# The pooled output projection of the first block in three fp32r products of halves, in place of plain fp32 products

## The chip, the cores and the metric

One core of one Trainium2 chip runs the whole program. The metric is the device time of one execution in microseconds (us). Times of single instructions come from one profiled execution on the chip.

## The reference

Two blocks run one after the other over 256 tokens of width 1024, each with two layers, all in fp32. The change lies in the first block, whose layer is (cut):

```python
proj = xm @ w_in[l]
q, k, v, u_pool, ga, gp = jnp.split(proj, splits, axis=-1)
...
attn = blocked_bidirectional_gqa(q, k, v) @ w_attn_o[l]
pool = multiscale_pool(u_pool, pool_mix_w[l], pool_scale[l]) @ w_pool_o[l]
merged = jax.nn.sigmoid(ga) * attn + jax.nn.sigmoid(gp) * pool
x = x + g1[:, None, :] * (merged @ w_out[l])
xf = modulate(rms_norm(x, norm_ffn_w[l]), sh2, sc2)
x = x + g2[:, None, :] * peer_ffn(xf, w_query[l], sub_keys[l], expert_u[l], expert_v[l])
```

`multiscale_pool` ends with four products of 128x128 (`pool_mix_w`, one for each group of 128 features) and a scale; its 512 features then go through `w_pool_o` (512 x 1024). That last product is the one that changes. `peer_ffn` picks 16 experts a token for each of 8 heads out of 16384 and gathers their rows.

## The kernel before

Activations lie transposed: 128 features on the partitions, 256 tokens along the free axis, so a matrix of width 1024 is 8 tiles of 128x256 (`KD` = 8). The weights of a layer come as one stream of 128x128 tiles, eight tiles (512 KB) to a chunk, into a ring of 7 chunks (`RING`). SyncE loads a chunk when TensorE has used the one 7 before it (`w_used`). The last 17 chunks of a layer don't go through the ring but into `spare` places, tiles whose first use is over by then (`load_spare`), and four (`EARLY`) into the rows' buffer.

A projection g fills one of four PSUM banks of `G` (`bank(g)`) and is taken out (evacuated) by another engine before the bank is used again (`bank_free_1`, `g_free`). It is made in one of two ways:

- `project` (L684): plain fp32 matmuls of the ring's tiles with the fp32 activations, `kt` of them. In the trace an fp32 matmul is two records.
- `project_halved` (L696, the products in `halved_products`, L354): weights and activations are each cut in a high half, rounded to fp32r, and a low half, the remainder, and three fp32r matmuls are added: high by high, high by low, low by high. ScalarE writes `w_high` of a whole chunk (`high_half`, L342), VectorE subtracts it from the ring's chunk into `w_low` (`low_half`, L350). There are three places for these halves (`PARTS`), so ScalarE waits until TensorE has used the halved chunk three before.

`HALVING_1` is the list of which projections are halved and so which chunks. `Halves.ahead(eng, g)` lets an engine cut all halved chunks up to two behind the last chunk of projection g. Each engine's order is written out by hand: it calls `ahead` at the head of each iteration.

The order of a layer on TensorE: 32 input projections (`ORDER_1`, halved but for v, mixed with the attention), chunks 0 to 31; four mixing products (`G_MIX`, one plain matmul each) of the `pooled` tiles that GpSimd made; eight pooled output projections (`G_POOLO`, four k-steps each, plain; tiles 260 to 291, in chunks 32 to 36); `ada_part`, 8 thin matmuls with one column; eight attention output projections (`G_ATTO`, halved, eight k-steps); eight of `w_out` (`G_OUT`, halved); the norm, the first expert queries, and the expert stage.

Around the change the other engines do this:

- ScalarE copies the mixing products out with the pool's scale (`mixed`, L933, shown as rows<-G,par), makes the high halves of the eight attention tiles (`x_high`, L992), then the `w_high` that `ahead` asks for.
- VectorE runs a loop over the eight pooled output projections: `ahead`, `x_low` of attention tile j (L1268), the merge of gate and projection j (L1290, shown as rows<-gates,G), which frees the bank, and one ada step (L450 or L452), a multiply-add of 128x1024 of the modulation weights. Layer 0 has ada steps here; layer 1 has none left (`STEPS` is 32, all taken in the input projections).
- TensorE's first attention output projection waits for `x_low` tile by tile.
- The places: `pooled` and `mixed` lie in the rows' buffer, behind them the padded inputs of the pool (`upad`, `win`). The first four `spare` places lie on those, too.

Of the kernel before, what the change touches and what calls it, by code (L numbers as in the profile page):

```python
# [17 lines left out]
ALU = mybir.AluOpType  # L18
ACT = mybir.ActivationFunctionType
AX_X = mybir.AxisListType.X  # L20
F32 = mybir.dt.float32
# [356 lines left out]
def halved_pair(pe, w, T, sem, halving, outs, high, low, kt, ready, full, place=UNSHIFTED):  # L378
# [5 lines left out]
    for ks in (range(split), range(split, kt)):  # L384
        for turn, out in enumerate(outs):
# [15 lines left out]
            if ks[-1] == kt - 1:  # L401
# [7 lines left out]
                    + [((4, False), G_POOLO + _j) for _j in range(KD)]  # L409
# [48 lines left out]
def first_layer(nc, layer, io, T, sem, rows, run, nxt):  # L458
# [55 lines left out]
    with block:  # L514
        @block.sync
        def _(sp):
# [15 lines left out]
            def load_spare(first, last):  # L532
                for n in range(first, last):
                    sp.dma_start(T["spare"][n], T["stream1"][layer * CHUNKS_1 + RING_CHUNKS + n]
                                 ).then_inc(run["c_then_spare_loaded"], 16)
# [9 lines left out]
            for at in range(EARLY[0] - RING, EARLY[0]):  # L545
                sp.wait_ge(sem["w_used"], at - RING + 1)
                load_chunk(sp, T["stream1"], layer, CHUNKS_1, ring, sem["w_loaded"], at)
                if at == EARLY[0] - RING:
                    sp.wait_ge(sem["pooled"], 4)
                    load_spare(0, 4)  # L550
                if at == EARLY[0] - RING + 2:
                    sp.wait_ge(sem["x_low_ready"], 2 * KD)
                    load_spare(4, 6)
                if at == EARLY[0] - RING + 3:
                    evacuated_1(sp, g_free, G_POOLO + KD - 1)
                    load_spare(6, 8)
# [105 lines left out]
        def _(pe):  # L662
# [33 lines left out]
            def project_halved(g, high, low, ready=None):  # L696
                bank_free_1(pe, g_free, g)
                halved_products(pe, w, T, sem, HALVING_1, G[:, bank(g), 0:S], high, low, KD, ready
                                ).then_inc(g_full, 1)
# [100 lines left out]
            for j in range(KD):  # L800
                project(G_POOLO + j, lambda k: mixed[:, k, :], 4)
# [127 lines left out]
        def _(act):  # L929
# [117 lines left out]
            for g in range(4):  # L1047
                copy_out(G_MIX + g, mixed[:, g, :], scale=columns(par, PAR_1, "pool_scale")[:, g:g + 1])
            act.wait_ge(sem["o_ready"], HEADS)
# [99 lines left out]
        def _(dve):  # L1149
# [123 lines left out]
            for i, what in enumerate(ORDER_1):  # L1273
# [8 lines left out]
                if i - 3 in q_at:  # L1282
                    maxima(q_at[i - 3])
            for j in range(KD):
# [1319 lines left out]
def second_layers(nc, io, T, sems, run):  # L2604
# [4 lines left out]
    with nc.Block() as block:  # L2609
# [22 lines left out]
        def _(dve):  # L2632
# [8 lines left out]
           "diag_ready", "y_copied", "dve_chain", "high_ready", "low_ready", "x_high_ready", "x_low_ready", "x2_high")  # L2641
# [41 lines left out]
def program(nc, io):  # L2683
    with ExitStack() as ctx:
# [34 lines left out]
        with ExitStack() as first:  # L2719
# [54 lines left out]
            with ExitStack() as scope_halves:  # L2774
# [4 lines left out]
                sb1("pooling_place", 6144)  # L2779
# [257 lines left out]
```

## Time and profile before

| what | us |
|---|---|
| median of 3 runs | 3457.57 (3456.27 to 3458.91) |
| the profiled execution | 3455.86 |
| its span, first to last instruction | 3454.1 |
| TensorE busy | 3175.4 (92%) |
| VectorE busy | 2464.8 (71%) |
| ScalarE busy | 1665.6 (48%) |
| GpSimd busy | 1142.0 (33%) |

The profile has 48307 instructions. Layer 0 of the first block lasts until about 964 us, layer 1 until about 1883, the second block the rest. In the 40 slices of the page TensorE is at nine tenths or more in nearly all of the second block. The DMA engines move about 409 GB/s in the expert stages and less elsewhere. A record of TensorE overlaps the next one, since its end is modelled; the distance between the starts tells what one costs. An entry such as "[5.61 <-ACT x_high L992]" says how long the engine was idle before the instruction, and what it waited for last.

### The profile page before, as it was taken

What the parts mean: (1) busy time and instruction counts of PE and PEld (TensorE: products, weight loads), DVE (VectorE), ACT (ScalarE), POOL (GpSimd) and SP (SyncE); (2) the same over time, 40 slices, a digit from 0 to 9 for tenths busy, and PEclk for the clock granted to TensorE, in tenths of its full rate; (3) what the DMA queues carried; (4) which work ended last, traced back from release to release, by engine and by line L of the source; (5) the groups of instructions that cost most, each with busy time, mean ns of one, the idle gap of its engine ahead of it and who ended that gap; (6) DMA issues with size and microseconds to landing.
All of it is one profiled execution on the core that took longest, in us unless ns stands there. A gap on an engine that the chain in (4) does not pass through costs nothing. (4 is left out here: it accounts for less than half of the span.)

```text
span 3454.1 us, 48307 instructions
## 1 busy us (share of the span) xinstructions
PE 3175.4 (92%) x16922; PEld 2418.2 (70%) x16922; DVE 2464.8 (71%) x4772; ACT 1665.6 (48%) x3730; POOL 1142.0 (33%) x1243
## 2 busy tenths in 40 slices
PE   6998999987789798988977999999999999999999
PEld 6995544443289764444423888999988888999988
DVE  7876776666577666677764877767787867867686
ACT  3743343333365433333333555756554655756553
POOL 1306677777613167777773000002000000002000
PEclk8999999999999899999999999999999999999999
DMA  8798999999966799999997554444455554444455
GB/s 309 241 352 346 409 409 409 408 408 409 394 245 201 286 409 409 409 408 407 406 409 291 176 183 141 136 144 137 159 187 185 182 184 141 136 141 140 159 187 161
DMA packets 258286, 936.98 MB, mean 271 GB/s; under 512 B 29312, under 2 KB 30720, under 8 KB 257792
## 3 DMA queue, kind: packets, MB, share of 16 engines
q0 software_dynamic: 161280, 587.27, 43.3%
q1 hardware_dynamic: 96768, 346.62, 30.4%
q8 instruction: 138, 2.26, 0.3%
q14 instruction: 100, 0.82, 0.1%
HBM read 932.73 MB, written 1.05 MB: 270 GB/s over the span
## 5 line engine op out<-in xcount | busy, mean ns | idle before, releaser
L876 PE MATMUL M<-rows,diag 128*128 128x512 f32 x2048 | 965.1, 609 | 179.1 <-DMA rows<-in_expert_v_dram,expert 164.5
L1398 DVE CUSTOM_DVE_ANT_0 rows<-rows,G 128x1024 f32<-128x1024 f32 x512 | 615.5, 1219 | 408.0 <-DMA rows<-in_expert_u_dram,expert 319.4
L876 PEld LDWEIGHTS M<-rows,diag 128*128 128x128 f32 x2048 | 368.1, 191 | 724.2 <-DMA rows<-in_expert_v_dram,expert 383.1
L350 DVE TENSOR_TENSOR w_low<-ring,w_high 128x1024 fp32r<-128x1024 f32 x560 | 689.9, 1235 | 246.5 <-ACT w_high L342 227.5
L342 ACT ACTIVATE w_high<-ring 128x1024 fp32r<-128x1024 f32 x560 | 590.6, 1057 | 251.9 <-PE G L433 134.0
L595 POOL DMA_INDIRECT rows<-in_expert_u_dram,expert x512 | 484.0, 945 | 326.8 <-DVE expert L1381 139.4
L595 POOL DMA_INDIRECT rows<-in_expert_v_dram,expert x512 | 482.3, 942 | 189.6 <-issue 117.0
L369 PE MATMUL G<-x_halves,w_high 128*128 128x256 f32 x1360 | 400.7, 295 | 4.1 <-DVE w_low L350 3.9
L372 PE MATMUL G<-x_halves,w_low 128*128 128x256 f32 x1360 | 386.0, 284 | 0.0
L1106 ACT ACTIVATE diag<-const,weight 128x128 f32<-128x128 f32 x512 | 197.0, 394 | 258.0 <-PE M L876 257.1
L371 PE MATMUL G<-x_halves,w_high 128*128 128x256 f32 x1104 | 314.5, 285 | 0.0
L1093 ACT ACTIVATE gelu<-hid 128x2 f32<-128x2 f32 x256 | 51.7, 202 | 483.4 <-DVE hid L1398 482.8
L369 PEld LDWEIGHTS G<-x_halves,w_high 128*128 128x128 f32 x1360 | 262.0, 193 | 12.2 <-issue 10.7
L1675 POOL TENSOR_TENSOR gates<-gates 128x256 f32<-128x256 f32 x30 | 22.2, 739 | 740.7 <-ACT xs L2079 740.7
L372 PEld LDWEIGHTS G<-x_halves,w_low 128*128 128x128 f32 x1360 | 261.9, 193 | 0.0
L433 PE MATMUL G<-ff_halves,w_high 128*128 128x512 f32 x672 | 239.3, 400 | 0.0
L433 PE MATMUL G<-x_halves,w_high 128*128 128x512 f32 x616 | 224.7, 403 | 12.9 <-DVE w_low L350 12.1
L433 PE MATMUL G<-attn_halves,w_high 128*128 128x512 f32 x616 | 221.6, 396 | 0.0
L371 PEld LDWEIGHTS G<-x_halves,w_high 128*128 128x128 f32 x1104 | 213.9, 194 | 0.9
L369 PE MATMUL G<-x_high,w_high 128*128 128x256 f32 x608 | 180.3, 296 | 15.6 <-DVE x_low L1268 14.1
L435 PE MATMUL G<-ff_halves,w_low 128*128 128x256 f32 x672 | 188.2, 280 | 0.0
L371 PE MATMUL G<-x_low,w_high 128*128 128x256 f32 x608 | 174.8, 287 | 0.0
(416 smaller groups left out, 6126.4 us busy)
## 6 DMA issues: line engine op xcount, KB each, us to landing
ring<-in_stream_dram SPq DMA_DIRECT2D x612, 512.0 KB, 3.5
ada_ring<-in_ada_stream_dram POOLq DMA_DIRECT2D x80, 512.0 KB, 5.2
rows<-in_ada_stream_dram POOLq DMA_DIRECT2D x16, 512.0 KB, 16.3
rows<-in_stream_dram SPq DMA_DIRECT2D x16, 512.0 KB, 7.4
rows<-in_expert_u_dram,expert POOLq DMA_INDIRECT x512, 10.5
rows<-in_expert_v_dram,expert POOLq DMA_INDIRECT x512, 10.5
ada_ring<-in_stream_dram SPq DMA_DIRECT2D x8, 512.0 KB, 6.7
spare<-in_stream_dram SPq DMA_DIRECT2D x6, 512.0 KB, 10.3
```

The costliest lines, as they stand in the source:

```text
L342: act.activation(T["w_high"][:, place.part(n), :], T["ring"][:, slot, :], ACT.Copy).then_inc(sem["high_ready"], 1)
L350: dve.tensor_tensor(T["w_low"][:, part, :], T["ring"][:, place.slot(chunk, slots), :], T["w_high"][:, part, :].bitcast(F32), ALU.subtract) ...
L369: mm = pe.matmul(out, T["w_high"][:, part, tile], high(k), start=(k == 0), stop=False)
L371: pe.matmul(out, T["w_high"][:, part, tile], low(k), start=False, stop=False)
L372: mm = pe.matmul(out, T["w_low"][:, part, tile], high(k), start=False, stop=(k == kt - 1))
L433: mm = pe.matmul(out, T["w_high"][:, part, tile], pair(k), start=(k == 0), stop=False)
L435: pe.matmul(out[:, 0:S], T["w_low"][:, part, tile], pair(k)[:, 0, :], start=False, stop=False)
L595: pool.indirect_dma_start(buf[:, n % SLOTS, :], None, table, bass.IndirectOffsetOnAxis(ap=T["expert"][:, r, k:k + 1], axis=0)).then_inc(la ...
L876: mm = pe.matmul(M[:, 2 * t + half, :], T["diag"][:, n % 4, :], T["v_rows"][:, n % SLOTS, half * 512:(half + 1) * 512], start=(h == 0 and ...
L1093: act.activation(T["gelu"][:, r, k0:k0 + PAIR], T["hid"][:, r, k0:k0 + PAIR], ACT.Gelu).then_inc(sem["gelu_done"], 1)
L1106: act.activation(T["diag"][:, n % 4, :], ident, ACT.Copy, scale=T["weight"][:, r, k:k + 1]).then_inc(sem["diag_ready"], 1)
L1398: dve.tensor_tensor_reduce(row, row, TOKENS, 1.0, 0.0, ALU.mult, ALU.add, T["hid"][:, r, k:k + 1]).then_inc(sem["u_used"], 1)
```

## The change

The pooled output projections become halved ones. Their weights' chunks 32 to 35 join the halved chunks (36 was one already, since the attention output projection shares it). The mixed tiles get halves: ScalarE makes `mixed_high` of a group right behind its copy, once the copy has ended, and VectorE makes `mixed_low` of the four groups ahead of its loop. TensorE's first pooled output projection waits for `mixed_low` tile by tile. Both halves lie where `upad` and `win` were, and so on the first two spare places; these first four spare loads move on the SyncE queue from behind the first of the last seven ring chunks before the early ones to behind the fourth.

```diff
@@ HALVING_1
-                    + [((4, False), G_POOLO + _j) for _j in range(KD)]
+                    + [((4, True), G_POOLO + _j) for _j in range(KD)]
@@ sync
-                if at == EARLY[0] - RING:
-                    sp.wait_ge(sem["pooled"], 4)
-                    load_spare(0, 4)
                 if at == EARLY[0] - RING + 2:
                     sp.wait_ge(sem["x_low_ready"], 2 * KD)
                     load_spare(4, 6)
                 if at == EARLY[0] - RING + 3:
                     evacuated_1(sp, g_free, G_POOLO + KD - 1)
+                    load_spare(0, 4)
                     load_spare(6, 8)
@@ tensor
-            def project_halved(g, high, low, ready=None):
+            def project_halved(g, high, low, ready=None, kt=KD):
                 bank_free_1(pe, g_free, g)
-                halved_products(pe, w, T, sem, HALVING_1, G[:, bank(g), 0:S], high, low, KD, ready
+                halved_products(pe, w, T, sem, HALVING_1, G[:, bank(g), 0:S], high, low, kt, ready
                                 ).then_inc(g_full, 1)
...
             for j in range(KD):
-                project(G_POOLO + j, lambda k: mixed[:, k, :], 4)
+                project_halved(G_POOLO + j, lambda k: T["mixed_high"][:, k, :], lambda k: T["mixed_low"][:, k, :],
+                               (lambda k: pe.wait_ge(sem["mixed_low_ready"], k + 1)) if j == 0 else None, 4)
@@ scalar
             for g in range(4):
                 copy_out(G_MIX + g, mixed[:, g, :], scale=columns(par, PAR_1, "pool_scale")[:, g:g + 1])
+                evacuated_1(act, g_free, G_MIX + g)
+                act.activation(T["mixed_high"][:, g, :], mixed[:, g, :], ACT.Copy).then_inc(sem["mixed_high_ready"], 1)
@@ vector
+            for g in range(4):
+                dve.wait_ge(sem["mixed_high_ready"], g + 1)
+                dve.tensor_tensor(T["mixed_low"][:, g, :], mixed[:, g, :], T["mixed_high"][:, g, :].bitcast(F32),
+                                  ALU.subtract).then_inc(sem["mixed_low_ready"], 1)
             for j in range(KD):
                 halves_of.ahead(dve, G_POOLO + j)
@@ program
-                sb1("pooling_place", 6144)
+                sb1("pooling_place", 2048)
+                T1["mixed_high"], T1["mixed_low"] = sb1("mixed_high", 4, S, dt=F32R), sb1("mixed_low", 4, S, dt=F32R)
+                sb1("padded_place", 2048)
```

The order on VectorE in layer 0, from the last w_low of the input projections (chunk 31) to the third merge, before:

```order
L350 TENSOR_TENSOR w_low<-ring,w_high 128x1024 [waits high_ready_a,ada_step_or_dta_ready_a]
L452 SCALAR_TENSOR_TENSOR query<-ada_ring,c_act,query 128x1024 [waits ada_loaded1]
L452 SCALAR_TENSOR_TENSOR query<-ada_ring,c_act,query 128x1024 [waits ada_loaded2,ada_step_or_dta_ready_a]
L452 SCALAR_TENSOR_TENSOR query<-ada_ring,c_act,query 128x1024 [waits ada_loaded3,ada_step_or_dta_ready_a]
L1268 TENSOR_TENSOR x_low<-attn,x_high 128x256 [waits x_high_ready_a,ada_step_or_dta_ready_a]
L1290 SCALAR_TENSOR_TENSOR rows<-gates,G 128x256 [waits g_full_a,g_free0_a]
L450 TENSOR_TENSOR query<-ada_ring,c_act 128x1024 [waits ada_loaded0,ada_full_or_acum_full_a]
L1268 TENSOR_TENSOR x_low<-attn,x_high 128x256 [waits x_high_ready_a,ada_step_or_dta_ready_a]
L1290 SCALAR_TENSOR_TENSOR rows<-gates,G 128x256 [waits g_full_a,g_free1_a]
```

And with the change (from the ada step behind that w_low; the merge is now L1295):

```order
L452 SCALAR_TENSOR_TENSOR query<-ada_ring,c_act,query 128x1024 [waits ada_loaded1]
L350 TENSOR_TENSOR w_low<-ring,w_high 128x1024 [waits high_ready_a,ada_step_or_dta_ready_a]
L452 SCALAR_TENSOR_TENSOR query<-ada_ring,c_act,query 128x1024 [waits ada_loaded2]
L350 TENSOR_TENSOR w_low<-ring,w_high 128x1024 [waits high_ready_a,ada_step_or_dta_ready_a]
L452 SCALAR_TENSOR_TENSOR query<-ada_ring,c_act,query 128x1024 [waits ada_loaded3]
L1287 TENSOR_TENSOR mixed_low<-rows,mixed_high 128x256 [waits mixed_high_ready_or_rot_full_a,ada_step_or_dta_ready_a]
L1287 TENSOR_TENSOR mixed_low<-rows,mixed_high 128x256 [waits mixed_high_ready_or_rot_full_a] x3
L350 TENSOR_TENSOR w_low<-ring,w_high 128x1024 [waits high_ready_a]
L1269 TENSOR_TENSOR x_low<-attn,x_high 128x256 [waits x_high_ready_a]
L1295 SCALAR_TENSOR_TENSOR rows<-gates,G 128x256 [waits g_full_a,g_free0_a]
L450 TENSOR_TENSOR query<-ada_ring,c_act 128x1024 [waits ada_loaded0,ada_full_or_acum_full_a]
L350 TENSOR_TENSOR w_low<-ring,w_high 128x1024 [waits high_ready_a,ada_step_or_dta_ready_a]
```

Four w_low (chunks 32 to 35) and four mixed_low are new. Two w_low stand between the last ada steps of the input projections, one (chunk 34) ahead of the first x_low and the first merge, one (chunk 35) at the head of the second iteration.

The order on ScalarE in layer 0, from the last attention tile to the w_high behind the x_high, before:

```order
L933 ACTIVATE gates<-G 128x256 [waits g_full_a] x2
L933 ACTIVATE rows<-G,par 128x256 [waits g_full_a] x4
L992 ACTIVATE x_high<-attn 128x256 [waits o_ready_a]
L992 ACTIVATE x_high<-attn 128x256 x7
L342 ACTIVATE w_high<-ring 128x1024 [waits w_used_a,w_loaded1_a]
```

And with the change, from the first copy of mixed (now L932) on:

```order
L932 ACTIVATE rows<-G,par 128x256 [waits g_full_a]
L1049 ACTIVATE mixed_high<-rows 128x256 [waits g_free0_a]
L932 ACTIVATE rows<-G,par 128x256 [waits g_full_a]
L1049 ACTIVATE mixed_high<-rows 128x256 [waits g_free1_a]
L932 ACTIVATE rows<-G,par 128x256 [waits g_full_a]
L1049 ACTIVATE mixed_high<-rows 128x256 [waits g_free2_a]
L932 ACTIVATE rows<-G,par 128x256 [waits g_full_a]
L1049 ACTIVATE mixed_high<-rows 128x256 [waits g_free3_a]
L991 ACTIVATE x_high<-attn 128x256 [waits o_ready_a]
L991 ACTIVATE x_high<-attn 128x256 x7
L342 ACTIVATE w_high<-ring 128x1024 [waits w_used_a,w_loaded6_a]
L342 ACTIVATE w_high<-ring 128x1024 [waits w_used_a,w_loaded0_a]
```

Before this piece, the w_high of chunks 32 and 33 now stand ahead of the last two gate copies. The copies of mixed alternate with the mixed_high, each of which waits for its copy, and the w_high of chunks 34 and 35 stand behind the eight x_high, ahead of those of 36 to 38.

## Rows read from the trace of the kernel before

**Rows 1.** The page, part 4: chain that ended last, by engine.

```profile
PE 41%; DVE 2%; ACT 1%; issue 1%; DVEq 0%; ACTq 0%
```

**Rows 2.** Busy time of two stretches of layer 0: A:B, length, each engine, PEclk, DMA.

```profile
178.29:192.18 13.89, 13.89 (x64) 12.27 (x65) 12.06 (x17) 5.14 (x11) 2.64 (x5) 1.00 0.89 313
197.76:221.30 23.54, 23.54 (x197) 23.54 (x198) 19.81 (x35) 10.11 (x15) 0.53 (x1) 1.00 0.94 351
```

**Rows 3.** TensorE in order of time, layer 0: start, us, instruction [idle before].

```profile
178.29 14.05 PE L691 MATMUL G<-rows,ring 128*128 128x256 f32 x64 [0.77 <-ACT rows L933]
192.18 1.84 PE L678 MATMUL M<-one,query 128*128 128x1 f32 x16
197.76 0.39 PE L369 MATMUL G<-x_high,w_high 128*128 128x256 f32 x1 [1.12 <-DVE x_low L1268]
```

**Rows 4.** ScalarE in order of time, layer 0; first the duration of the mixed copies.

```profile
L933 ACT ACTIVATE rows<-G,par x4: 473/474/475, 176.3 to 177.6; 128x256 f32<-128x256 f32 x4
...
172.96 0.38 ACT L933 ACTIVATE gates<-G 128x256 f32<-128x256 f32 x1 [2.49 <-PE G L372]
176.27 1.77 ACT L933 ACTIVATE rows<-G,par 128x256 f32<-128x256 f32 x4
177.94 2.54 ACT L992 ACTIVATE x_high<-attn 128x256 fp32r<-128x256 f32 x8
180.38 1.99 ACT L342 ACTIVATE w_high<-ring 128x1024 fp32r<-128x1024 f32 x2
```

**Rows 5.** VectorE in order of time, layer 0.

```profile
168.91 3.92 DVE L452 SCALAR_TENSOR_TENSOR query<-ada_ring,c_act,query 128x1024 f32<-128x1024 f32 x3
178.44 0.43 DVE L1268 TENSOR_TENSOR x_low<-attn,x_high 128x256 fp32r<-128x256 f32 x1 [5.61 <-ACT x_high L992]
180.37 0.42 DVE L1290 SCALAR_TENSOR_TENSOR rows<-gates,G 128x256 f32<-128x256 f32 x1 [1.50 <-PE G L691]
...
182.31 0.41 DVE L1290 SCALAR_TENSOR_TENSOR rows<-gates,G 128x256 f32<-128x256 f32 x1
...
184.29 0.42 DVE L1290 SCALAR_TENSOR_TENSOR rows<-gates,G 128x256 f32<-128x256 f32 x1
...
187.41 0.41 DVE L1290 SCALAR_TENSOR_TENSOR rows<-gates,G 128x256 f32<-128x256 f32 x1
...
197.29 0.42 DVE L1268 TENSOR_TENSOR x_low<-attn,x_high 128x256 fp32r<-128x256 f32 x1
```

**Rows 6.** ScalarE, VectorE and TensorE in order of time, layer 1.

```profile
1099.86 1.77 ACT L933 ACTIVATE rows<-G,par 128x256 f32<-128x256 f32 x4
...
1107.76 0.42 DVE L1290 SCALAR_TENSOR_TENSOR rows<-gates,G 128x256 f32<-128x256 f32 x1 [1.31 <-PE G L691]
...
1115.79 0.42 DVE L1268 TENSOR_TENSOR x_low<-attn,x_high 128x256 fp32r<-128x256 f32 x1
...
1115.77 1.84 PE L678 MATMUL M<-one,query 128*128 128x1 f32 x16
1117.48 0.37 PE L369 MATMUL G<-x_high,w_high 128*128 128x256 f32 x1
```

**Rows 7.** TensorE in order of time, and stretches with the granted clock (last but two).

```profile
1003.02 1.84 PE L678 MATMUL M<-one,query 128*128 128x1 f32 x16
...
1170.73 2.04 PE L854 MATMUL G<-xm,ring 128*128 128x128 f32 x8 [2.55 <-ACT xm L1075]
...
283.75 6.64 PE L876 MATMUL M<-rows,diag 128*128 128x512 f32 x8 [14.66 <-ACT diag L1106]
...
1006.50:1010.00 3.50, 3.50 (x19) 3.50 (x18) 3.09 (x5) 0.62 (x1) 0.07 (x1) 0.51 0.78 287
1170.50:1174.00 3.50, 3.27 (x16) 3.30 (x17) 3.47 (x14) 3.50 (x11) 0.00 (x0) 0.53 1.03 411
...
288.00:292.00 4.00, 4.00 (x13) 2.43 (x12) 3.51 (x8) 0.40 (x2) 3.01 (x4) 0.78 1.03 411
```

**Rows 8.** DMA issues of SyncE between 217 and 220: KB each, us to landing.

```profile
ring<-in_stream_dram SPq DMA_DIRECT2D x1, 512.0 KB, 9.1
```

More of the change, by code:

```diff
@@ L2640 @@
            "pooled", "merged", "top_ready", "gate_exp", "routed", "u_used", "v_used", "gelu_done", "weight_ready", "gate_normed",
-           "diag_ready", "y_copied", "dve_chain", "high_ready", "low_ready", "x_high_ready", "x_low_ready", "x2_high")
+           "diag_ready", "y_copied", "dve_chain", "high_ready", "low_ready", "x_high_ready", "x_low_ready", "x2_high",
+           "mixed_high_ready", "mixed_low_ready")
 NAMES_2 = ("par_loaded", "w_used", "g_full", "sq_ready", "norm_full", "std_ready", "rstd_ready", "xm_ready",
```

## The prediction

> **What bounds the kernel now.** I read the chain that ended last first. TensorE holds 41% of the span on it and VectorE 2%; the rest of the share lies in the expert stage, where gathers pace the kernel [rows 1]. So a microsecond that TensorE loses in the projections of the first block is a microsecond of the end, as long as nothing idles behind it. Next the busy time of the stages around the change in layer 0. In the stage of the pooled output projection (178.29 to 192.18) TensorE is busy all 13.89 us, and in the 23.54 us from 197.76 on it never idles either, at granted clock 1.00 [rows 2]. The gap between the two is the place to look at. TensorE's order of time shows it [rows 3]: 64 records of the plain fp32 projection in 13.89 us, 1.70 us of one-column matmuls for the ada part, then the first attention projection, whose eighth k-step waits 1.12 us for x_low of VectorE. From 197.76 everything runs without a gap. That x_low is thus what releases the stage, and the time at which VectorE issues it decides.
>
> VectorE in the same stretch [rows 5] idles 5.61 us ahead of its first x_low at 178.44, starts its first merge at 180.37, when TensorE has the first result, and is packed from there: x_low, merge and an ada step take 1.98 us an iteration (182.31 to 184.29), and 3.12 us where a w_low of a chunk stands in it (184.29 to 187.41), so a w_low costs 1.14 us of VectorE's order. Seven iterations, three of them with a w_low, bring it from 180.37 to the last x_low at 197.29. VectorE bounds this stage, not TensorE, although TensorE is the busy one. In layer 1 there is no ada step in the loop: there the merges wait for TensorE (1.31 us at 1107.76), the last x_low starts at 1115.79, before TensorE's one-column matmuls are done, and the attention projection starts at 1117.48 on TensorE's own time [rows 6].
>
> **The products themselves.** A plain fp32 product is two records: 13.89 us over 32 products is 0.434 us each [rows 3]. An fp32r product takes 0.12 us: 197 of them start in the 23.54 us from 197.76 [rows 2]; three take 0.36 us. 32 times 0.074 us is 2.4 us less TensorE work a layer. The trace says that the saving is 17%. The Trainium skill, FP8 and Floating Point Precision, TensorE Precision Notes, says that true FP32 takes four passes of the array, and three products in place of four passes would save 25%, some 3.5 us a layer; the trace disagrees with that as a time, since an fp32r product costs 0.12 us and not a quarter of 0.434. By the page's rule layer 1 below would come out some 0.7 us lower.
>
> **What is added.** Four more chunks a layer, 32 to 35, are halved: four w_high on ScalarE and four w_low on VectorE. Besides, four mixed_high of 128x256 and four mixed_low. The chunks 32 and 33 now fall under the last two gate projections of the main loop. Their w_high stand in ScalarE's gaps of some 2.5 us ahead of the gate copies there (172.96 [rows 4]), the second from 173.2 to 174.3. Their w_low take VectorE up to: ada step at 168.91, w_low, ada step, w_low behind its w_high at 174.4, ada step to 176.8. That is inside the idle stretch before 178.44 [rows 5] and costs nothing; without that cover it would be 2.3 us a layer.
>
> ScalarE [rows 4]: four copies of mixed in 1.77 us, then the eight x_high at 177.94, then w_high at 180.38 (two in 1.99 us, about 1.06 one alone). Now each copy must have ended before its mixed_high starts: 0.474 of a copy plus a hand-over of some 0.03 (an estimate) plus 0.31 for the high half (2.54 over 8) is 0.81 us a pair, 3.25 us for four in place of 1.67. So the x_high start 1.6 us later, at 179.5, and the w_high of chunk 34 runs from 182.0 to 183.05. TensorE starts the projection when the fourth copy is out (179.2 against 178.29), its fourth k-step waits for the fourth mixed_low until 180.15, and the first three projections are done near 183.7: the fourth needs chunk 34.
>
> VectorE, layer 0: the w_low of chunk 34 stands ahead of the first x_low and the first merge in its order. It starts at 183.13 (w_high's end and about 0.1 us of hand-over, an estimate: the first x_low started 0.5 us behind the start of the first x_high, which takes 0.3 to 0.4), the first merge therefore at 183.13 + 1.14 + 0.34 = 184.6 where it was 180.37: 4.24 us later. Then the w_low of chunk 35 comes into the second iteration: 1.14 more. The rest of the loop is what it was, iteration by iteration. The last x_low is 5.38 us later, at 202.7, and with it TensorE's eighth k-step (203.15 for 197.76). Behind that point TensorE had no gap [rows 2] and VectorE's work lies as before relative to it, so all of it goes on to the end: **+5.4 us** in layer 0. The 2.4 us of TensorE work saved turns into waiting for banks and for x_low.
>
> Layer 1, with the copies at 1099.86 [rows 6], the same shift against layer 0 of 923.59: w_low of chunk 34 is done at 1107.95, and TensorE goes on with the fourth projection at 1108.0. The merges, without ada steps, free the banks in time (the fourth at 1112.9, needed at 1113.8). Five projections of 12 products at 0.12 us bring it to 1115.2, the one-column matmuls to 1116.9, against 1117.48: **-0.6 us**. Bounds: -1.4 if the wait for chunk 34 is not there (start 1.0 later, 2.4 saved), +1.0 if the w_low of chunks 35 and 36 hold back the banks by a further iteration.
>
> The SyncE queue: four of the 512 KB spare loads leave their place behind the chunk loaded at 206 and follow three ring chunks later. The ring chunk then issued at 217.26 landed 9.1 us later [rows 8], and up to four loads can now crowd ahead of it; what was ahead of it before is the same total unless the DMA engines run empty in between. I take 0 and keep +1 as the bound. The changed semaphore names cost nothing, they are the same waits.
>
> **The sum.** 5.4 - 0.6 = +4.8 us, bounds +3.3 and +6.4 (0.2 us on each of the eight hand-overs, layer 1's bounds in part, the queue). The profiled execution took 3455.86 us (span 3454.1), 1.7 below the median of 3457.57; against it the sum is 3460.7, and against the median, by which I predict, **3462.4 us**.
>
> **The rivals.** *The clock falls.* In layer 0 TensorE is now nearly idle from 198.5 to 203.15: only the seventh k-step, 0.36 us at 200.1, and its columns before were the thin ada matmuls. The trace shows what little activity does. After 2.55 us of idling at 1170.73 the granted clock was 0.53 over 1170.5 to 1174, and the one-column matmuls at 1003.02 (1.84 us) were followed by 0.51 over 1006.5 to 1010, with TensorE packed [rows 7]. At 283.75, after 14.66 us, it worked at half speed up to within 288 to 292, where the mean was 0.78, so to about 289.8. Half speed (1.2 for 2.4 GHz) after resuming thus lasts 3.0 to 6.0 us and costs 1.5 to 3.0, middle 2.3: 4.8 + 2.3 = +7.1, **3464.7 us**, slower by over 0.2%. It decides if the fall comes before or just after 203.15. Against it: in the old gap of 1.12 us, with the thin matmuls before it, the clock stayed at 1.00. The Trainium skill, TensorE: Matmul & The Clock Gate, Part 1, has the same: idling returns the array to the lower of two rates; rows 7 agree. Chance 0.25.
>
> *The chain is covered.* If VectorE does not order itself as I say, for instance since the w_high of chunk 34 comes ahead of the x_high, TensorE's saving shows: at most 2.4 less a later start of 1.0, so -1.4 a layer, -2.8 in all, **3454.8 us**. For it speaks only that TensorE is 100% busy in the stage; against it the order on ScalarE and VectorE. Chance 0.1. Even the whole saving of both layers, -4.8, is within 0.2%.
>
> *The products do not get cheaper*: fp32r products with waits between them at more than 0.12 us. In layer 0 VectorE hides it; in layer 1 at 0.145 the gain is gone, so +6 at most. Chance 0.1, within the range.
>
> **How the numbers follow.** Forecast 0.5, clock 0.25, covered 0.1, dearer products 0.1, anything else 0.05. A measurement of this kernel tells about 0.2%, 6.9 us, from no change. The forecast lies below that, the clock's case on both sides of it with two thirds above, so slower 0.24, same 0.74, faster 0.02. The range runs from 3457.5 (the forecast's low bound and part of what lies between it and the covered case) to 3466.0 (the clock's case at 3.0 plus 0.7 for the rest).
>
> **What would show it.** Layer 0: first merge near 184.6, the last x_low near 202.7, a wait of TensorE for x_low of over 2 us, attention projections from 203.1 on without a gap. ScalarE's x_high near 179.5. Layer 1: attention projection at 1116.9 plus layer 0's shift. Wrong if the first merge of layer 0 starts before 182, if the granted clock falls in the 10 us behind 200, or if TensorE waits for a ring chunk in the output projection.

## The result, and the profile after

| kernel | median, us | range | runs |
|---|---|---|---|
| before | 3457.44 | 3455.73 to 3459.79 | 16 |
| changed | 3464.64 | 3463.60 to 3466.92 | 16 |

The ratio is 1.0021, 95% interval 1.0014 to 1.0027: the change costs 7.2 us, just over 0.2%, the size from which a difference of this kernel counts as one here. The forecast was +4.8 (3462.4), the rival in which the clock falls +7.1 (3464.7), the range 3457.5 to 3466.0.

The profiled execution took 3464.55 us (span 3462.7). TensorE is busy for 3175.1 us, as before, VectorE for 2476.0 (11 more), ScalarE for 1677.4 (12 more). The chain of the page doesn't change in its first row, against [rows 1]:

```profile
PE 41%; DVE 2%; ACT 1%; issue 1%; DVEq 0%; ACTq 0%
```

So the page doesn't show where 7.2 us went; the order of time in the two layers does. TensorE, layer 0, against [rows 3] (everything here starts 0.61 us later, which arose before the first copy and is no part of the change's section; this execution also had a stretch at the lower clock between 80 and 88 us, mean 0.79, where the one before had 1.00):

```profile
180.10 0.35 PE L369 MATMUL G<-mixed_high,w_high 128*128 128x256 f32 x1 [1.97 <-DVE mixed_low L1287]
185.05 0.36 PE L369 MATMUL G<-mixed_high,w_high 128*128 128x256 f32 x1 [0.41 <-DVE w_low L350]
...
193.78 0.39 PE L369 MATMUL G<-mixed_high,w_high 128*128 128x256 f32 x1 [1.42 <-DVE rows L1295]
195.33 1.84 PE L676 MATMUL M<-one,query 128*128 128x1 f32 x16
200.55 0.39 PE L369 MATMUL G<-x_high,w_high 128*128 128x256 f32 x1 [1.12 <-DVE x_low L1269]
203.67 0.58 PE L369 MATMUL G<-x_high,w_high 128*128 128x256 f32 x1 [2.50 <-DVE x_low L1269]
204.05 0.41 PE L371 MATMUL G<-x_low,w_high 128*128 128x256 f32 x1
204.26 0.41 PE L372 MATMUL G<-x_high,w_low 128*128 128x256 f32 x1
```

TensorE's waits between 176 and 230 us (waiting line, what it waited for: us in total, times, longest), where before there were 1.1 us for x_low and 0.8 for rows:

```profile
PE G L369 <- DVE x_low L1269: 3.6, 2, 2.5
PE G L369 <- DVE rows L1295: 2.3, 3, 1.4
PE G L369 <- DVE mixed_low L1287: 2.0, 1, 2.0
PE G L369 <- DVE w_low L350: 0.4, 1, 0.4
```

By their names all four are on VectorE. The one of 2.0 us is not: a wait for several semaphores is put down to the last that came, and ahead of its first pooled output projection TensorE waits for all four copies (`evacuated_1` for each `G_MIX` bank, as in the kernel before, where that wait was 0.77 us and had ScalarE's name). The first low half, all that the first product needs, was done at 178.32 (below); the fourth copy ended at 179.79, and TensorE went on at 180.10. Where the text goes on calling it the wait for mixed_low, that is the profile's name for it.

ScalarE in order of time, layer 0, against [rows 4]: a copy and a high half alternate, 0.82 us from copy to copy, and x_high and w_high follow.

```profile
176.88 0.47 ACT L932 ACTIVATE rows<-G,par 128x256 f32<-128x256 f32 x1
177.38 0.42 ACT L1049 ACTIVATE mixed_high<-rows 128x256 fp32r<-128x256 f32 x1
177.71 0.46 ACT L932 ACTIVATE rows<-G,par 128x256 f32<-128x256 f32 x1
...
179.33 0.46 ACT L932 ACTIVATE rows<-G,par 128x256 f32<-128x256 f32 x1
...
180.14 2.55 ACT L991 ACTIVATE x_high<-attn 128x256 fp32r<-128x256 f32 x8
182.60 1.99 ACT L342 ACTIVATE w_high<-ring 128x1024 fp32r<-128x1024 f32 x2
```

VectorE, against [rows 5]: the first mixed_low, then a wait of 2.98 us for that w_high, with x_low and merge queued behind.

```profile
177.90 0.42 DVE L1287 TENSOR_TENSOR mixed_low<-rows,mixed_high 128x256 fp32r<-128x256 f32 x1 [0.48 <-ACT mixed_high L1049]
...
183.68 1.23 DVE L350 TENSOR_TENSOR w_low<-ring,w_high 128x1024 fp32r<-128x1024 f32 x1 [2.98 <-ACT w_high L342]
184.82 0.42 DVE L1269 TENSOR_TENSOR x_low<-attn,x_high 128x256 fp32r<-128x256 f32 x1
185.15 0.41 DVE L1295 SCALAR_TENSOR_TENSOR rows<-gates,G 128x256 f32<-128x256 f32 x1
...
203.20 0.42 DVE L1269 TENSOR_TENSOR x_low<-attn,x_high 128x256 fp32r<-128x256 f32 x1
```

The clock, against [rows 2]: stretches of the changed kernel with the granted clock last but two.

```profile
200.00:204.00 4.00, 0.95 (x4) 0.75 (x5) 3.93 (x8) 0.00 (x0) 1.06 (x2) 0.85 0.86 287
204.00:208.00 4.00, 4.00 (x20) 4.00 (x20) 3.29 (x5) 0.45 (x1) 0.53 (x1) 0.50 0.72 227
208.00:212.00 4.00, 4.00 (x30) 4.00 (x30) 2.32 (x4) 1.50 (x3) 0.00 (x0) 0.80 0.62 201
212.00:216.00 4.00, 4.00 (x36) 4.00 (x35) 2.94 (x5) 2.14 (x4) 0.00 (x0) 1.00 0.59 158
```

TensorE resumes at 203.67 at the lower of its two levels (1.2 GHz) and stays there until about 209.6 (0.80 over four microseconds is 1.6 at half). The starts are 0.213 us apart where they were 0.12.

Layer 1, against [rows 6]: ScalarE, then TensorE.

```profile
1108.50 0.47 ACT L932 ACTIVATE rows<-G,par 128x256 f32<-128x256 f32 x1
...
1116.66 0.36 PE L369 MATMUL G<-mixed_high,w_high 128*128 128x256 f32 x1 [0.37 <-DVE w_low L350]
1123.92 1.84 PE L676 MATMUL M<-one,query 128*128 128x1 f32 x16
1125.63 0.36 PE L369 MATMUL G<-x_high,w_high 128*128 128x256 f32 x1
```

The attention projection starts 17.13 us behind the first copy, 17.62 before: 0.49 sooner.

**A ledger by sections.** What happens elsewhere in 3.4 ms scatters by 1 or 2 us between executions, so each layer is read as a section: from the start of the first copy of mixed to the start of `std` on ScalarE, behind the ffn norm. These are its ends before:

```profile
246.85 0.47 ACT L958 ACTIVATE std<-M,eps 128x256 f32<-128x256 f32 x1 [2.45 <-PE M L705]
...
1168.21 0.47 ACT L958 ACTIVATE std<-M,eps 128x256 f32<-128x256 f32 x1 [2.52 <-PE M L705]
```

and after:

```profile
255.34 0.47 ACT L957 ACTIVATE std<-M,eps 128x256 f32<-128x256 f32 x1 [2.45 <-PE M L703]
...
1176.36 0.47 ACT L957 ACTIVATE std<-M,eps 128x256 f32<-128x256 f32 x1 [2.52 <-PE M L703]
```

Layer 0: 246.85 - 176.27 = 70.58 us before, 255.34 - 176.88 = 78.46 after, +7.88. Layer 1: 68.35 and 67.86, -0.49. Together +7.39, beside 7.2 by the medians. The two profiled executions themselves are 8.69 us apart (3464.55 and 3455.86); the 1.3 us that the sections don't hold lie elsewhere, 0.61 of them before the first copy. Every run below has its two sections read in the same way, from one profiled execution each, which need not be a typical one: that of e_one_ahead was the slowest of its 11 (3465.41 us, median 3461.85), that of e_direct the slowest but one (3463.20, median 3461.36).

| kernel | layer 0 | first merge / last x_low after the first copy | layer 1 | median, us |
|---|---|---|---|---|
| before | 70.58 | 4.10 / 21.02 | 68.35 | 3457.44 |
| changed | 78.46 | 8.27 / 26.32 | 67.86 | 3464.64 |
| e_after_again | 78.07 | 8.27 / 26.32 | 67.88 | 3463.74 |
| e_layer0 | 77.10 | as changed | 68.36 (plain) | 3463.68 |
| e_layer1 | 70.57 (plain) | as before | 68.74 | 3458.33 |
| e_loads | 70.57 | as before | 68.35 | 3457.36 |
| e_tiny_before | 69.20 | 4.10 / 16.36 | 68.35 | 3457.41 |
| e_tiny_after | 69.75 | 8.27 / 20.19 | 67.86 | 3458.17 |
| e_one_ahead | 77.85 | 5.00 / 23.33 | 67.86 | 3461.85 |
| e_busy | 75.88 | 8.27 / 26.31 | 68.73 | 3463.31 |
| e_busy_both | 75.88 | 8.28 / 26.32 | 67.87 | 3464.55 |
| e_direct_layer1 | 70.59 (plain) | as before | 66.27 | 3456.44 |
| e_direct | 76.96 | 6.68 / 24.73 | 66.28 | 3461.36 |
| e_first34_layer1 | 70.58 (plain) | as before | 65.32 | 3454.98 |

The kernel before, run beside them, had medians of 3457.0 to 3457.7.

### The profile page after: what moved, and what is told of

It reads as the page before. It is cut to its first block and busy times, and to the rows that moved or that the text cites. A ratio compares the mean times of both kernels' runs of the same rounds, so it can differ in the third digit from the quotient of the medians.

```text
span 3462.7 us, 48483 instructions
## 1 busy us (share of the span) xinstructions
PE 3175.1 (92%) x16986; PEld 2418.5 (70%) x16986; DVE 2476.0 (72%) x4788; ACT 1677.4 (48%) x3746; POOL 1143.8 (33%) x1243
## 5 line engine op out<-in xcount | busy, mean ns | idle before, releaser
L350 DVE TENSOR_TENSOR w_low<-ring,w_high 128x1024 fp32r<-128x1024 f32 x568 | 699.5, 1235 | 259.0 <-ACT w_high L342 240.2
L342 ACT ACTIVATE w_high<-ring 128x1024 fp32r<-128x1024 f32 x568 | 599.2, 1057 | 252.8 <-PE G L433 133.8
```

What stands on the lines that cost most here:

```text
L342: act.activation(T["w_high"][:, place.part(n), :], T["ring"][:, slot, :], ACT.Copy).then_inc(sem["high_ready"], 1)
L350: dve.tensor_tensor(T["w_low"][:, part, :], T["ring"][:, place.slot(chunk, slots), :], T["w_high"][:, part, :].bitcast(F32), ALU.subtract) ...
```

## The experiments

The theory: in layer 0 VectorE's order, pushed back by ScalarE's pairs and by w_low of chunks 34 and 35, costs some 5.3 us, layer 1 gives 0.5 back, and the clock that falls in the longer wait costs the rest. The rivals: the moved spare loads, dearer products, or the clock alone.

**One layer at a time, and the loads alone.** In e_layer0 and e_layer1 the chunks are halved, and the new products made, in one layer only (the list below is of e_layer0; e_layer1 has it the other way round), and the spare loads are moved in both; e_loads is the kernel before with nothing but the moved spare loads.

```diff
-HALVING_1 = Halving(...)
+POOL_HALVED = (True, False)
+HALVINGS = [halving_of(_cut) for _cut in POOL_HALVED]
+    HALVING_1, cut_pool = HALVINGS[layer], POOL_HALVED[layer]
...
+                if not cut_pool:
+                    project(G_POOLO + j, lambda k: mixed[:, k, :], 4)
+                    continue
```

> The change in layer 0 alone; layer 1 keeps its plain fp32 pooled output projection (and the moved spare loads). Theory 1: layer 0 costs 5.4 us of VectorE's order and about 2.4 of the clock, layer 1 gains 0.5; so layer 0 alone is +7.7 us, 3465.1 us, slower than the changed kernel by 0.5. Theory 2 (the cost is common to both layers, from products with waits between them or from the moved loads): about half, +3.6 us, 3461.0.

> The change in layer 1 alone, where no ada steps stand in VectorE's loop. Theory 1: -0.5 us against the kernel before, 3456.9 us, since TensorE saves 2.4 and gives back 1.1 at the later start and 0.9 at the wait for the low half of chunk 34. Theory 2: about half of the cost, +3.6 us, 3461.0.

> The kernel before with only the move of the four spare loads on the SyncE queue. Theory 1: no change, 3457.4, within 0.5. Theory 2 (part of the +7.2 is the crowding of loads ahead of the ring's chunks in the output projections): +1 to +2 us, with TensorE or ScalarE waiting for a ring chunk between 225 and 245.

Measured: e_layer0 3463.68 us, ratio 1.0019 (1.0010 to 1.0028); e_layer1 3458.33, 1.0003 (0.9994 to 1.0012); e_loads 3457.36, 1.0000 (0.9991 to 1.0009). The loss is in layer 0, and the loads are worth nothing: both sections of e_loads are those of before to 0.01 us. Layer 1 alone doesn't differ measurably from before. Its section took 68.74, 0.39 more than before and not 0.49 less, since in this execution the clock fell behind the wait of 2.0 us for mixed_low, 0.6 us after TensorE had resumed at 1101.32:

```profile
1100.00:1104.00 4.00, 2.68 (x15) 2.71 (x16) 1.14 (x3) 3.94 (x13) 0.00 (x0) 0.75 0.32 70
1104.00:1108.00 4.00, 4.00 (x30) 4.00 (x30) 3.11 (x5) 2.22 (x3) 0.00 (x0) 0.83 0.66 199
```

That wait is in both layers of the changed kernel, and behind it the clock fell in some executions and not in others (layer 1: here and in e_busy, not in the other four that have it: the changed kernel, its repetition, e_tiny_after and e_one_ahead). In layer 0 such a fall is hidden, as VectorE ends later anyway (e_after_again and e_busy had one there). I had not looked for it.

**VectorE's order, lighter.** The ada steps in the loop of layer 0 work on 8 of 1024 columns, in the kernel before and in the changed one. This leaves out most of what these steps add to the modulation.

```diff
-                ada_steps(1)
+                ada_steps(1, 8)
```

> The kernel before, with the eight ada steps of layer 0's loop over the pooled output projections cut to 8 of their 1024 columns (so that part of the modulation is wrong). VectorE's loop then looks like layer 1's. Theory 1: TensorE no longer waits for x_low, the 1.12 us wait at 197.76 and its restart go, -1.4 us, 3455.8.

> The changed kernel with the same ada steps cut to 8 columns (part of the modulation is left out). Theory 1 (VectorE's order is what costs in layer 0): layer 0 now behaves as layer 1, each gains 0.5 or, where the clock falls in TensorE's 2 us wait for mixed_low, loses 0.4; so 3454.8 to 3456.6, 8 to 9 us below the changed kernel and within 1 us of the same edit on the kernel before. Theory 2 (dearer products, later loads): it stays 5 to 7 us above it, near 3462.

Measured: 3457.41 us (1.0001, 0.9992 to 1.0010) and 3458.17 (1.0003, 0.9994 to 1.0012). The medians alone can't tell these from before; the sections can. The changed layer 0 takes 69.75 us in place of 78.46, and the change costs 0.55 us (69.75 against 69.20) where it cost 7.88, though the first merge is as late as ever (8.27). TensorE then waits for VectorE once between 174 and 220 us:

```profile
PE G L369 <- DVE mixed_low L1287: 2.0, 1, 2.0
```

So it isn't the products, the halves or the hand-overs by themselves; it is that they stand in a VectorE order that was already full. The 0.55 includes half clock over most of 180 to 184 behind that wait; layer 1, with the same order and no fall, has -0.49. The expected difference between the two medians, under 1 us, came out (0.76), but each expected median was missed by 1.5 us or more, on the high side: of the 1.38 us that e_tiny_before gains in its section nothing shows in its median.

**One w_low later.** VectorE cuts weights ahead by one chunk and not by two.

```diff
-                halves_of.ahead(dve, G_POOLO + j)
+                halves_of.ahead(dve, G_POOLO + j, 1)
```

> The changed kernel with VectorE cutting chunks only one ahead instead of two in its loop over the pooled output projections: the low half of chunk 34 stands behind the first merge, and that of chunk 38 behind the last x_low. Theory 1: the first merge of layer 0 starts near 181.4 + 0.6 instead of 185.15, the last x_low some 3 us earlier (near 200.2), of which TensorE gives back up to 1 while it waits for later low halves; the time is 3462.6 if the clock still falls in layer 0, 3460.1 if it no longer does. Theory 2 (TensorE's own products or the transfers set the end of the stage): no change, 3464.6.

Measured: 3461.85 us (1.0013, 1.0004 to 1.0022). The last x_low comes 3.0 us sooner, and the section is 0.6 us shorter only. TensorE now waits for w_low:

```profile
185.35 0.35 PE L369 MATMUL G<-mixed_high,w_high 128*128 128x256 f32 x1 [0.47 <-DVE w_low L350]
190.46 0.36 PE L369 MATMUL G<-mixed_high,w_high 128*128 128x256 f32 x1 [2.00 <-DVE w_low L350]
195.56 0.36 PE L369 MATMUL G<-mixed_high,w_high 128*128 128x256 f32 x1 [2.01 <-DVE w_low L350]
197.91 3.41 PE L676 MATMUL M<-one,query 128*128 128x1 f32 x16
```

It gets to the one-column matmuls 20.79 us behind the first copy (18.45 in the changed kernel), and the clock has fallen by then, at 195.98, 0.4 us after TensorE had resumed: they take 3.41 us in place of 1.84.

```profile
192.00:200.00 8.00, 5.99 (x36) 5.82 (x35) 7.86 (x12) 1.07 (x1) 2.02 (x4) 0.75 0.90 311
200.00:204.00 4.00, 4.00 (x20) 4.00 (x20) 3.78 (x6) 0.00 (x0) 0.62 (x2) 0.50 0.76 258
```

Half clock lasts until about 206.2, 10.2 us with TensorE at work, the longest fall in any of these sections. It reaches the eighth k-step at 205.81 and waits for no x_low, though the last one had started at 200.45: in this execution TensorE at half clock set the end of the stage, no longer VectorE. By the 0.44 us that a microsecond at half clock costs (worked out below) that is some 4.5 us, an estimate, and without it the section would be about 73.4, near the 3.0 us that x_low comes sooner (the 75.88 us that the section of the changed order takes without a fall, below, less 3.0 are 72.9). And the profiled execution was the slowest of the 11: by the medians the kernel is 2.8 us faster than the changed one, 1.9 than its repetition. So the lighter order probably does give back most of the 3 us, and the clock takes a part of it that differs from execution to execution; one profile doesn't settle how much.

**The clock.** Dummy products fill TensorE's waits. They read halves that are there, write to a bank that nothing reads at that time, and do no part of the work. In e_busy they stand ahead of the seventh and eighth k-step in layer 0, in e_busy_both also ahead of the first pooled output projection (the wait of 2.0 us) in both layers.

```diff
+            def warm_ready(k):
+                if opening and k in (6, 7):
+                    for _ in range(8 if k == 6 else 20):
+                        pe.matmul(SC[:, 0:S], T["w_high"][:, HALVING_1.number[37] % PARTS, 0:P], x_high(0), ...)
+                pe.wait_ge(sem["x_low_ready"], KD + k + 1)
```

> The changed kernel, with 28 extra fp32r products of 128x256 on TensorE in layer 0, which write a bank that nobody reads (8 ahead of the seventh k-step of the first attention output projection, 20 ahead of the eighth), so that TensorE works while it waits for x_low. Theory 1 (VectorE's order costs 4.9 us, the fall of the clock behind the wait the other 2.3): the granted clock stays at 1.00 from 200 to 215 us, and the time falls from 3464.6 by 2.3 us to 3462.3, though TensorE has 3.4 us more work. Theory 2 (the whole +7.2 is order and transfers, the clock is only a companion): no change, 3464.6, or slower by what the extra products stick out of the waits, up to 1 us.

> The change with two sets of dummy products, which write to a bank that nothing reads there: 28 in layer 0's waits for x_low, and 16 in both layers ahead of the wait for the first low half of mixed. They do no part of the work. Theory that the chain of halves costs 5.3 us in layer 0 and the clock the rest: the granted clock stays at 1.00 from 184 to 216 in layer 0 and from 1104 to 1120 in layer 1, layer 0 takes 75.8 to 76.0 us (5.3 more than before), layer 1 67.8 (0.5 less), the kernel 4.8 above the one before, about 3462. Rival, that the dummy products only shift the fall: it comes back somewhere in the two sections and they take 77 or more and 68.3 or more. Rival, that the wait for x_low is made longer by TensorE's own work: last x_low later than 26.32 after the first copy.

> The changed kernel once more, unedited, to see how steady its ledger is. From the first copy of mixed to the ffn norm's std layer 0 took 78.46 us in the first profile (7.88 more than before) and layer 1 67.86 (0.49 less). Theory of the chain of halves plus the clock: VectorE's times against the first copy come out the same to 0.1 us (first merge +8.27, last x_low +26.32), and only the time at half clock behind the wait for x_low differs; with 3.4 us of it layer 0 takes about 76.7 to 77.2, with 6.8 us 78.4. The kernel 5 to 7.5 us above the one before. Rival, that the order of the shared queues makes it: the time from the copies to the last x_low itself would vary by 1 us or more.

Measured: e_busy 3463.31 us (1.0019, 1.0010 to 1.0028), e_busy_both 3464.55 (1.0020, 1.0011 to 1.0029), e_after_again 3463.74 (1.0018, 1.0009 to 1.0027). TensorE in e_busy_both, where M is the dummies' bank, and the granted clock:

```profile
198.16 1.12 PE L771 MATMUL M<-x_high,w_high 128*128 128x256 f32 x8
...
199.91 2.56 PE L771 MATMUL M<-x_high,w_high 128*128 128x256 f32 x20
202.58 0.39 PE L369 MATMUL G<-x_high,w_high 128*128 128x256 f32 x1
```

```profile
200.00:204.00 4.00, 3.90 (x33) 3.69 (x32) 3.96 (x5) 0.00 (x0) 0.53 (x1) 1.00 0.86 299
204.00:208.00 4.00, 4.00 (x36) 4.00 (x35) 3.90 (x8) 1.76 (x3) 0.53 (x1) 1.00 0.77 245
```

The clock stays at 1.00 there, x_low is as late as in the changed kernel (26.32), and layer 0 takes 75.88 us in both runs: +5.30, VectorE's part alone. Layer 1 takes 67.87. With the two waits for x_low filled the fall is gone, so what is over 75.88 is the clock's: 2.58 us in the changed kernel, 2.19 in its repetition, 1.22 in e_layer0. In e_layer0 TensorE was back at full clock by 206.6, 2.8 us after it resumed at 203.77:

```profile
204.00:208.00 4.00, 4.00 (x25) 4.00 (x26) 3.39 (x6) 0.72 (x1) 0.53 (x1) 0.68 0.69 221
```

The dummies don't tell which idling brings the fall, since they fill both waits. It isn't the length of the 2.50 us alone: in e_after_again the clock had fallen by 201.5, 0.7 us into that wait (200.79 to 203.29), where the kernel before kept it at 1.00 through 1.12 us. Ahead of it lay in all four a wait of 1.4 us for a bank, 12 products, 16 one-column matmuls, 18 products, a wait of 1.1 and three products; that this idling counts as well is likely, and no run shows it by itself.

The whole kernel doesn't show this saving of 2 us: e_busy's median is 0.4 us below that of e_after_again, e_busy_both's is 0.8 above it and as high as the changed kernel's, against an expected 3462, and the intervals are 6 us wide. In the profiled execution of e_busy_both the two sections are 4.82 us above before, and the rest of the kernel 1.9 us longer by its span; the second block, which nothing here touches, is 2.4 us longer, the rest between a little shorter. That scatter stays unexplained. The clock's cost is therefore shown in the section, not in the kernel's time.

**Halves straight from the bank.** ScalarE writes the high half of mixed from the PSUM bank with the scale, and VectorE the low half as bank times scale less the high half, so the four copies are not made. TensorE's wait for all four banks goes with them: its first product waits for the first low half only.

```diff
-            for g in range(4):
+            for g in range(0 if cut_pool else 4):
                 evacuated_1(pe, g_free, G_MIX + g)
...
-                copy_out(G_MIX + g, mixed[:, g, :], scale=...)
-                evacuated_1(act, g_free, G_MIX + g)
-                act.activation(T["mixed_high"][:, g, :], mixed[:, g, :], ACT.Copy)...
+                act.activation(T["mixed_high"][:, g, :], G[:, bank(G_MIX + g), 0:S], ACT.Copy, scale=...)...
...
+                dve.scalar_tensor_tensor(out=T["mixed_low"][:, g, :], in0=G[:, bank(G_MIX + g), 0:S],
+                                         scalar=..., in1=T["mixed_high"][:, g, :], op0=ALU.mult, op1=ALU.subtract)
```

e_direct_layer1 does so with the change in layer 1 alone, e_direct in both layers. e_first34_layer1 is e_direct_layer1 with one line more, ahead of the x_high loop, so that w_high of chunk 34 comes first: `halves_of.ahead(act, G_POOLO)`.

> The change in layer 1 alone, and there without the mixed copy: ScalarE writes mixed_high straight from the bank with the pool's scale, VectorE takes mixed_low as bank times scale minus the high half. ScalarE's four instructions then follow each other at 0.43 us again, TensorE's first pooled projection starts about 1.2 us earlier than with the copy and has under 1 us of idling ahead of it, so the clock holds. Theory 1: layer 1's section (copies to norm) takes 66.7 us where it was 68.35 before, the kernel -1.6 us against the kernel before, 3455.8. Rival: the low half of chunk 34 still holds TensorE back (w_high behind the eight x_high), then only -0.5 to -1.0.

> In both layers the high half of mixed is taken by ScalarE straight from the bank, and the low half by VectorE as bank times scale less the high half; mixed itself isn't written. This takes four copies of 0.35 to 0.47 us out of ScalarE's order ahead of the x_high halves. Theory that ScalarE's pairs of copy and half push w_high of chunk 34 and with it VectorE's order: in layer 0 the x_high start about 1.6 us earlier than in the changed kernel, the first merge comes 6.4 to 6.8 us after the first high half where it was 8.27, the last x_low about 24.6 for 26.32, and layer 0 takes 74.0 to 74.4 us plus 1.2 to 2.6 for the clock; layer 1 66.27 as in the run with the edit there alone. The kernel 1.4 to 4 us above the one before. Rival, that w_low of the chunks alone makes VectorE late: the last x_low stays at 26 us and layer 0 at 77 to 78.5.

> The change in layer 1 alone, with the high half of mixed straight from the bank, and ScalarE cuts chunk 34 ahead of the eight x_high halves. Theory that in layer 1 only the arrival of chunk 34's halves still makes TensorE wait (0.74 us at its fourth projection): that wait goes, and w_low of chunk 34 no longer holds back VectorE's first x_low; layer 1 takes 65.4 to 65.8 us from the first high half to the ffn norm's std, against 66.27 and 68.35, and the kernel is 2.5 to 2.9 us below the one before, about 3454.6. Rival: the x_high halves 1 us later become late for the attention projection, TensorE waits there for x_low instead, and layer 1 stays at 66.3 or above.

Measured: 3456.44 us (0.9999, 0.9990 to 1.0008), 3461.36 (1.0012, 1.0003 to 1.0021) and 3454.98 (0.9993, 0.9984 to 1.0002). ScalarE and VectorE of e_direct in layer 0:

```profile
176.33 1.77 ACT L1060 ACTIVATE mixed_high<-G,par 128x256 fp32r<-128x256 f32 x4
178.00 2.55 ACT L1000 ACTIVATE x_high<-attn 128x256 fp32r<-128x256 f32 x8
...
183.01 0.41 DVE L1309 SCALAR_TENSOR_TENSOR rows<-gates,G 128x256 f32<-128x256 f32 x1
...
201.06 0.42 DVE L1281 TENSOR_TENSOR x_low<-attn,x_high 128x256 fp32r<-128x256 f32 x1
```

The x_high start 1.67 us behind the first half, as behind the first copy before [rows 4], and with them the first merge and the last x_low come 1.59 us sooner than in the changed kernel: exactly what ScalarE's pairs had added. Still the last x_low is 3.71 us later than before, which is the w_low of two chunks and the wait for the first. 70.58 + 3.71 is 74.29; the other 2.67 us of the section's 76.96 go with half clock, from before TensorE resumed at 201.53 until 207.6. TensorE's first product starts 1.21 us behind the first half (3.22 in the changed kernel), and the wait of 2.0 us is gone in both layers, with no fall of the clock there; in layer 0 the time is lost again in the waits for w_low, banks and x_low.

In layer 1 the direct halves gain 2.08 us, which is 1.59 less than the changed kernel's section, again what the pairs cost: TensorE still waits 0.74 us there for the w_low of chunk 34. With chunk 34 first the gain is 3.03 (65.32 against 68.35), with no wait left on TensorE between 1095 and 1120. That is the best version found: 2.8 us below before by the medians, but the interval still holds no change. What the wait for four banks is worth by itself, no run tells; leaving it out of the changed kernel was not tried.

```profile
1101.00 1.77 ACT L1060 ACTIVATE mixed_high<-G,par 128x256 fp32r<-128x256 f32 x4
1102.69 1.07 ACT L342 ACTIVATE w_high<-ring 128x1024 fp32r<-128x1024 f32 x1
1103.66 2.54 ACT L1000 ACTIVATE x_high<-attn 128x256 fp32r<-128x256 f32 x8
```

## Why the prediction was right, and where it was off

- *Products at 0.12 us, a saving of 0.074 each.* Right. In layer 1 TensorE makes 60 products from 1116.66 to 1123.92, 0.121 each. The rival of dearer products falls. (Its price was a little low: 60 products at 0.145 in place of 0.12 are 1.5 us, so +6.3 and not +6 at most.) That the trace disagrees with four passes as a time says too much, though: 0.434 us is four times 0.1085, and 256 columns at 2.4 GHz are 0.107. What doesn't follow is the step from there to an fp32r product, which takes 0.120.
- *Chunks 32 and 33 cost nothing.* Right: behind their w_low VectorE ends its last ada step at 177.42 (176.14 and 1.28) and idles 0.48 us before the first mixed_low.
- *ScalarE's pairs at 0.81 us, x_high at 179.5, w_high of chunk 34 at 182.0.* Measured less the 0.61 of the later start: 179.53 and 181.99. e_direct confirms their share of 1.6 us. TensorE started at 179.49 and not 179.2, behind the fourth copy as the working says, and its fourth k-step had nothing to wait for then; neither mattered, as it waits for chunk 34 next.
- *VectorE in layer 0: first merge 184.6, last x_low 202.7, TensorE's resumption 203.15.* Measured, less 0.61: 184.54, 202.59, 203.06. The forecast +5.4 us is +5.30 where the clock is kept up (e_busy, e_busy_both), and e_tiny_after shows that the full order of VectorE is the cause.
- *Layer 1: -0.6.* Measured -0.47 to -0.49 in four of six executions (and -0.48 with dummies); with a fall of the clock behind the wait of 2.0 us +0.4, inside the bounds, through a mechanism that they did not name.
- *The queue: 0.* Right (e_loads).
- *The forecast of +4.8 as the likeliest case.* This is the step that failed. It took the granted clock as 1.00 behind 203.15, and gave the fall a chance of 0.25; the clock fell there in the changed kernel, in its repetition, in e_layer0 and in e_direct, each time within the wait of 2.50 us, 0.7 to 1.9 us after it began, and in neither run with the dummies in it. The row to weigh was there: 2.55 us of idling were followed by 0.53 [rows 7], while the argument against came from a gap of 1.12 us, less than half as long as the one that the working itself forecast. That the length of a gap is what decides is not shown: the fall 0.7 us into it, in e_after_again, speaks for the thin work ahead of it counting as well.
- *The price of the fall, 1.5 to 3.0 us, middle 2.3.* Measured in the sections 2.6, 2.2 and 1.2 (changed, repetition, e_layer0), and 2.7 in e_direct, there against a sum. The low end was too high: half clock lasted 5.9, 5.0, 2.8 and 6.1 us after TensorE resumed. And a microsecond at half clock costs 0.44 of a microsecond, not 0.5, since a product takes 0.213 us there and 0.120 at full clock ((0.213 - 0.120) / 0.213). By these the four prices come to 2.6, 2.2, 1.2 and 2.7. The Trainium skill, TensorE: Matmul & The Clock Gate, Part 1, says that start to start is the columns over 1.2 GHz at the lower rate, and at the higher one the columns over 2.4 GHz plus a small fixed cost; the trace agrees with the first (256 columns, 0.213 us) and shows 0.120 for the second, so 0.013 beyond the columns.
- *The chain is covered.* Fallen: VectorE and ScalarE ordered themselves as read.

The sum of what was measured in the sections is 5.30 + 2.58 - 0.49 = 7.39, and the medians say 7.2: the mechanism is the forecast's with the rival's on top. That the time is the rival's to 0.1 us is partly luck: the clock's price was 1.2 to 2.7 us from one profiled execution to the next, and the repetition's median lies only 6.0 us above the kernel before beside it.

## What to carry to other kernels

An engine that is 100% busy in a stage need not bound it: cheaper products on TensorE paid nothing in layer 0, because the halves they need were put into the order of the engine that released the stage. Lay out that engine's order instruction by instruction before the edit, and where the working ends in a stretch in which TensorE does little, look up what the clock did in such stretches: here it cost 1.2 to 2.7 us on top of the wait. Hold a profiled execution against the median of its kernel before reading a small edit's worth from it. Where the other engine has slack (layer 1), the same change gains, and more of it once the copy in front of the half is saved and the first weights are cut first.

## What was not expected of the hardware

- Behind the same wait of 2.0 us ahead of the pooled output projections the clock fell in five of twelve places (six executions' layer 0, six executions' layer 1), 0.6 to 1.3 us after TensorE had resumed, and stayed at 1.00 in the others. In the wait of 2.50 us it fell in all four that were profiled, but half clock lasted from 2.8 to 6.1 us after TensorE had resumed. A trace of one execution gives the mechanism, not the price.
- One-column matmuls slow down as well: 16 records took 3.41 us behind a fall and 1.84 otherwise, nearly the whole factor of two.
